# Two-layer streaming encoder: the slots of the weights' high and low parts at eight different residues of 128 bytes

## Chip, cores, metric

The kernel runs on one core of a Trainium2 chip. The metric is the device time of one execution in microseconds; lower is better.

## What is computed

The reference runs 1024 frames of width 1024, in float32, through two layers. The parts that take nearly all the time are products of activations with weights:

```python
h = h + mixer_ab(rmsnorm(h, g1), w_in, rel_a, sinks, w_out, t5_bias)   # layer 0: two kinds of chunked attention
h = h + dense_swiglu(rmsnorm(h, g2), wg, wu, wd)                       # 1024 -> 2816 -> 1024
h = h + mixer_c(rmsnorm(h, g1), w_in, vg, ws, bs, w_out)               # layer 1: gated unit with spatial mixing
h = h + moe_swiglu(rmsnorm(h, g2), wr, weg, weu, wed)                  # top 2 of 8 experts, 1024 -> 3584 -> 1024
return rmsnorm(h, final_norm)

def dense_swiglu(h, w_gate, w_up, w_down):
    return (jax.nn.silu(h @ w_gate) * (h @ w_up)) @ w_down
```

## The kernel before

**Split products.** Every float32 factor of a large product is split into a high part, rounded to `float32r`, and a low part, what the rounding left. A product is then three matmuls: high by high, high by low, low by high. `product` (line 306) writes them; all its matmuls carry line 314. Where its output is 512 columns wide and `wide` is not set, it does 256 columns at a time, and every matmul loads its stationary operand anew.

**Weights in units.** All weights come as units of 128 x 1024 floats. Four slots hold them: `wraw[:, j]` (as loaded), `wh[:, j]` (high part) and `wl[:, j]` (low part), j = 0 to 3. Unit u goes to slot u % 4. SyncE loads two slots at a time into `wraw` (`load_units`, line 286) once their low parts are made. ScalarE copies `wraw` to `wh` with rounding (`hi_part`, line 293, record at line 297), after the DMA and after TensorE is done with the unit that was in the slot (`unit_used`). VectorE subtracts (`lo_part`, line 299, record at line 301) and raises `lo_done`, for which TensorE waits before it uses the unit. There are 884 units in this run: 208 of the main weights and 676 of the experts.

**Who uses a unit, and how.**
- Projections (`half_pe` line 480, `out_unit_pe` line 855, `gate_up_pe` line 1120, `down_pe` line 1171): a tile of 128 x 128 of `wh` or `wl` is the stationary operand, and 240 to 512 columns of activations stream. These activations are `xs` (normalised input), `ah`/`al` (dense hidden), `exh`/`exl` (an expert's input) and `mah`/`mal` (an expert's hidden).
- The values of attention (`values_pe`, line 461) and of the gated unit (`mix_pe`, line 1290): 512 columns of `wh` or `wl` stream, and a tile of `xs` is stationary.
- The spatial mixing (in `mix_pe`) multiplies `wsh`/`wsl` with `vgh`/`vgl` by the same `product`, with 128 columns, and uses no unit.

**The stages in time.** Attention and its projections; output projection; dense layer in two halves of 512 frames (66 units each, 48 matmuls for each unit); gated unit; routing; then the items of the experts. An item is the frames of one expert, here eight of them, in rising order of size, each padded to a width out of `WIDTHS` (here three of 240, two of 256, two of 288, one of 304). An item takes 84 units: 56 for gate and up, 14 and 14 for the two halves of down, with 24 matmuls each.

**The allocation.** The tensors lie one behind the other in each partition. `wraw` begins at byte 16512, `wh` at 32896 and `wl` at 49280, all multiples of 128, and a slot has 4096 bytes. Then follow `ident`, `ones`, `gains` and other small ones, and from byte 67392 (64 past a multiple of 128) the large activations. `xs`, `ah`, `al`, `exh`, `exl`, `mah`, `mal`, `vgh`, `vgl`, `wsh` and `wsl` all begin 64 past a multiple of 128, and every slice that a matmul of line 314 takes keeps that. `eA` begins 64 past such a multiple too; `eB` begins 96 past one, and its second head 1028 bytes behind the first. Both are transposed with `ident` (lines 588 and 611).

Of the kernel before, what the change touches and what calls it, by code (L numbers as in the profile page):

```python
# [7 lines left out]
F32 = mybir.dt.float32  # L8
F32R = mybir.dt.float32r
U32 = mybir.dt.uint32  # L10
I32 = mybir.dt.int32
ALU = mybir.AluOpType
ACT = mybir.ActivationFunctionType
AX = mybir.AxisListType

P = 128
# [19 lines left out]
WIDTHS = (240, 256, 272, 288, 304, 336, CAP)  # L36
PIECES = -(-T // CAP)
NCAND = PIECES * NE
ROWS = 8
SLOTS = 2 * T + CAP  # L40


def t5_onehot():
# [15 lines left out]
def build(nc, io):  # L59
    ctx = ExitStack()  # L60
    with ctx:
        def sem(name):
            return ctx.enter_context(nc.semaphore(name))

        def sb(name, shape, dt=F32, scope=ctx):
            return scope.enter_context(nc.sbuf_tensor(name, shape, dt))


        wraw = sb("wraw", [P, 4, 1024])
        wh = sb("wh", [P, 4, 1024], F32R)  # L70
        wl = sb("wl", [P, 4, 1024], F32R)
        ident = sb("ident", [P, P])
        ones = sb("ones", [P, P])
        gains = sb("gains", [P, 4, KD])
# [4 lines left out]
        gate = sb("gate", [P, 2, NT])  # L79
        slot = sb("slot", [P, 2, NT], U32)  # L80
        tokl = sb("tokl", [P, CAP // P], U32)
        itab = sb("itab", [1, 3, NCAND + 1], I32)
        nitem = sb("nitem", [1, 1], I32)
        upto = sb("upto", [1, len(WIDTHS) + 1], I32)
        ps = ctx.enter_context(nc.psum_tensor("ps", [P, 8 * 512], F32))

        def bank(b, n=512, off=0):
# [80 lines left out]
        s4 = ExitStack()  # L168
# [25 lines left out]
        gt = sb("gt", [P, 3, NT], F32, s4)  # L194
        zlist = sb("zlist", [P, SLOTS // P], U32, s4)
        cand = sb("cand", [1, 6, NCAND], F32, s4)
        icnt = sb("icnt", [1, NCAND + 1], F32, s4)
        itf = sb("itf", [1, 3, NCAND + 1], F32, s4)
        s4.close()

        s4 = ExitStack()
# [5 lines left out]
        s4 = ExitStack()  # L207
# [5 lines left out]
        s4 = ExitStack()  # L213
# [5 lines left out]
        s4 = ExitStack()  # L219
# [17 lines left out]
        hrow_d = nc.dram_tensor("hrow_d", [T, D], F32)  # L237
        yrow_d = nc.dram_tensor("yrow_d", [SLOTS, D], F32)
        tok_d = nc.dram_tensor("tok_d", [SLOTS, 1], U32)
        extA_d = nc.dram_tensor("extA_d", [8, EXT_A], F32)  # L240
# [7 lines left out]
        hi_done, lo_done = sem("hi_done"), sem("lo_done")  # L248
# [44 lines left out]
        def hi_part(act, q, j):  # L293
            act.wait_ge(raw[j], 16 * q + 16)
            if not (isinstance(q, int) and q == 0):
                act.wait_ge(unit_used, 4 * q + j - 3)
            act.activation(wh[:, j], wraw[:, j], ACT.Copy).then_inc(hi_done, 1)  # L297

        def lo_part(dve, q, j):
            dve.wait_ge(hi_done, 4 * q + j + 1)  # L300
            dve.tensor_tensor(wl[:, j], wraw[:, j], wh[:, j].bitcast(F32),  # L301
                              ALU.subtract).then_inc(lo_done, 1)

        COLS = 256
# [367 lines left out]
        def first_act(act):  # L672
            act.wait_ge(tab_st, 80)
            for t in (0, 2):
                act.wait_ge(v_mm, t + 1)
                act.activation(vA[:, t], bank(t), ACT.Copy).then_inc(v_even, 1)
            for j in range(3):
                hi_part(act, 1, j)
            for t in (4, 6):
                act.wait_ge(v_mm, t + 1)  # L680
                act.activation(vA[:, t], bank(t), ACT.Copy).then_inc(v_even, 1)
            hi_part(act, 1, 3)
            half_act(act, U_KB, 0, 0)
            half_act(act, U_KB, 1, 1)
            hi_part(act, 2, 0)
            act.wait_ge(first_half, 2)
            act.activation(vbT[:, 0:HALF], bank(2), ACT.Copy).then_inc(pj_hi, 1)
            hi_part(act, 2, 1)
            half_act(act, unit_of(0, QA), 0, 4)
            act.wait_ge(vb_tr, 1)  # L690
            act.activation(vB[:, 0:4], bank(0).rearrange("p (t d) -> p t d", d=P), ACT.Copy).then_inc(vb_cp, 1)
            half_act(act, unit_of(0, KA), 0, 5)
            act.wait_ge(sink_in, 16)
            sink_act(act, 0)
            exps_a_act(act, 0)
            half_act(act, unit_of(0, QB), 0, 6)
            exps_b_act(act, 0)

        def first_dve(dve):
            dve.wait_ge(tab_st, 80)  # L700
            for t in (1, 3):
                dve.wait_ge(v_mm, t + 1)
                dve.tensor_copy(vA[:, t], bank(t)).then_inc(v_odd, 1)
            for j in range(3):
                lo_part(dve, 1, j)
            for t in (5, 7):
                if t == 5:
                    dve.wait_ge(v_mm, t + 1)
                else:
                    dve.wait_ge(unit_used, 4)  # L710
                dve.tensor_copy(vA[:, t], bank(t)).then_inc(v_odd, 1)
            lo_part(dve, 1, 3)
            half_dve(dve, U_KB, 0, 0, 0)
            half_dve(dve, U_KB, 1, 1, 1)
            lo_part(dve, 2, 0)
            dve.wait_ge(unit_used, U_VB + 1)
            dve.tensor_copy(vbT[:, HALF:T], bank(3)).then_inc(pj_lo, 1)
            lo_part(dve, 2, 1)
            half_dve(dve, unit_of(0, QA), 0, 4, 3)
            dve.wait_ge(vb_tr, 1)  # L720
            dve.tensor_copy(vB[:, 4:8], bank(1).rearrange("p (t d) -> p t d", d=P)).then_inc(vb_cp, 1)
            half_dve(dve, unit_of(0, KA), 0, 5, 4)
            least_a_dve(dve, 0)
            share_a_dve(dve, 0)
            half_dve(dve, unit_of(0, QB), 0, 6, 5)
            least_b_dve(dve, 0)
            share_b_dve(dve, 0)
# [991 lines left out]
        def item_act(act, it, n, base):  # L1719
            q = it * TURNS_E + Q_MOE  # L1720
            f0 = it * NF_E + F0
            gate_up_act(act, q, 0, NF_E, n, mah, f0, mst)
            d0, d1 = down_e(0), down_e(1)
            feed_act(act, q + d0[0], d0[1], NF_E // 2 - 1)
            copy_y_act(act, it, 0, n)
            turn_x_act(act, it + 1)
            feed_last_act(act, q + d0[0], d0[1], NF_E // 2)
            rows_y_act(act, it, 0, n, base)
            feed_act(act, q + d1[0], d1[1], NF_E // 2 - 1)
            copy_y_act(act, it, 1, n)  # L1730
            feed_last_act(act, q + d1[0], d1[1], NF_E // 2)
            rows_y_act(act, it, 1, n, base)
# [132 lines left out]
        def _(pool):  # L1865
# [75 lines left out]
            with pool.Fori(0, n_items) as it:  # L1941
                base = pool.value_load(itab[0:1, 1, bass.ds(it + 1, 1)], min_val=0, max_val=SLOTS - CAP)
                pool.wait_ge(xt_mm, 8 * it + 8)
# [26 lines left out]
        def _(act):  # L1970
# [24 lines left out]
            def item(it, n):  # L1995
                base = act.value_load(itab[0:1, 1, bass.ds(it, 1)], min_val=0, max_val=SLOTS - CAP)
                item_act(act, it, n, base)
# [112 lines left out]
```

## Time and profile before

| | before |
|---|---|
| time, median of 3 runs | 3727.32 us (3726.42 to 3730.49) |
| span of the profiled execution | 3722.7 us |
| PE busy | 3575.3 us, 96% |
| weight loads (PEld) busy | 3469.0 us, 93% |
| VectorE busy | 1769.7 us, 48% |
| ScalarE busy | 1672.4 us, 45% |
| GpSimd busy | 106.4 us, 3% |
| matmuls, weight loads | 29176 each |

The span runs from the first to the last instruction of one profiled execution; the median of the timed runs is 4.6 us longer. A busy share is not a rate: matmuls are pipelined, so several are shown as running at once, and how fast TensorE goes is seen from how many matmuls a stretch holds.

### The profile page before, as it was taken

The numbers are of one execution on the slowest core, as the hardware profiler recorded it, in microseconds if no ns is written. First come the engines' busy times: TensorE is split into PE (matmuls) and PEld (weight loads), VectorE is DVE, ScalarE is ACT, GpSimd is POOL, SyncE is SP. The second block draws the span as 40 slices with busy tenths as digits, with TensorE's granted clock in tenths as the row PEclk, the third lists the DMA queues.
The fourth block names the chain that finished last, engine by engine and source line by source line (L and its number), as shares of the span: only waits on it lengthen the run. The fifth ranks groups of instructions, "written<-read, shape, count | busy, mean of one in ns | idle before, by whom it ended". The sixth has DMA issues, their size and how long they took to land.

```text
span 3722.7 us, 76289 instructions
## 1 busy us (share of the span) xinstructions
PE 3575.3 (96%) x29176; PEld 3469.0 (93%) x29176; DVE 1769.7 (48%) x2532; ACT 1672.4 (45%) x2324; POOL 106.4 (3%) x137
## 2 busy tenths in 40 slices
PE   7999899999999999979999999999999999999993
PEld 5888799999999989879999999999999999999993
DVE  4455543333333455355555555555554444444444
ACT  3355533332333333346465564655644544544542
POOL 1000000000000000020000000000000000000001
PEclk9999999999999999979999999999999999999997
DMA  5111333333333322275666666566664555554446
GB/s 179 35 49 38 132 94 92 96 91 113 96 92 95 119 91 91 85 204 191 207 195 197 202 198 205 188 195 200 195 203 154 166 178 164 163 176 158 157 156 237
DMA packets 155604, 546.82 MB, mean 147 GB/s; under 512 B 18408, under 2 KB 18448, under 8 KB 155488
## 3 DMA queue, kind: packets, MB, share of 16 engines
q1 hardware_dynamic: 129744, 472.44, 40.0%
q0 software_dynamic: 16464, 55.52, 4.3%
q10 hardware_dynamic: 9280, 17.24, 1.2%
q8 instruction: 82, 1.34, 0.2%
q14 instruction: 34, 0.28, 0.0%
HBM read 515.51 MB, written 33.28 MB: 147 GB/s over the span
## 4 chain that ended last, share of the span: by engine, by line
PE 93%; DVE 3%; issue 1%; ACT 1%; DMA 1%; POOL 0%; ACTq 0%; DVEq 0%; POOLq 0%
PE ps L314 89%; DVE exl L1661 1%; PE ps L603 1%; PE ps L588 1%; PE ps L542 1%; PE ps L363 0%; DMA y<-yrow_d,slot 0%; PE ps L611 0%; PE ps L623 0%; PE ps L982 0%; PE ps L566 0%; DVE wl L301 0%; PE ps L1003 0%; ACT eA L662 0%; DMA yT<-in_xT 0%
## 5 line engine op out<-in xcount | busy, mean ns | idle before, releaser
L301 DVE TENSOR_TENSOR wl<-wraw,wh 128x1024 fp32r<-128x1024 f32 x884 | 1081.9, 1225 | 1442.6 <-ACT wh L297 1439.6
L297 ACT ACTIVATE wh<-wraw 128x1024 fp32r<-128x1024 f32 x884 | 929.4, 1057 | 1045.3 <-PE ps L314 1031.0
L314 PE MATMUL ps<-exh,wh 128*128 128x240 f32 (+3 forms) x3584 | 1020.6, 285 | 12.0 <-issue 9.8
L314 PE MATMUL ps<-exl,wh 128*128 128x240 f32 (+3 forms) x3584 | 1021.0, 285 | 0.0
L314 PE MATMUL ps<-exh,wl 128*128 128x240 f32 (+3 forms) x3584 | 1017.4, 284 | 0.0
L314 PE MATMUL ps<-xs,wh 128*128 128x256 f32 x5248 | 835.4, 282 | 2.4 <-DVE qAl L649 2.0
L314 PEld LDWEIGHTS ps<-xs,wh 128*128 128x128 f32 x5248 | 710.4, 190 | 12.5 <-issue 8.5
L314 PEld LDWEIGHTS ps<-exh,wh 128*128 128x128 f32 x3584 | 676.8, 189 | 13.1 <-issue 13.1
L314 PEld LDWEIGHTS ps<-exh,wl 128*128 128x128 f32 x3584 | 678.1, 189 | 0.0
L314 PEld LDWEIGHTS ps<-exl,wh 128*128 128x128 f32 x3584 | 677.7, 189 | 0.0
L314 PE MATMUL ps<-xs,wl 128*128 128x256 f32 x2624 | 521.6, 281 | 0.0
L314 PE MATMUL ps<-mah,wh 128*128 (+4 forms) x1792 | 510.4, 285 | 2.5 <-DVE exl L1661 2.5
L314 PE MATMUL ps<-mal,wh 128*128 (+4 forms) x1792 | 509.9, 285 | 0.0
L314 PE MATMUL ps<-mah,wl 128*128 (+4 forms) x1792 | 509.1, 284 | 0.0
L314 PEld LDWEIGHTS ps<-xs,wl 128*128 128x128 f32 x2624 | 402.5, 189 | 0.0
L314 PEld LDWEIGHTS ps<-mah,wh 128*128 128x128 f32 x1792 | 337.8, 189 | 4.4 <-issue 4.4
L314 PEld LDWEIGHTS ps<-mah,wl 128*128 128x128 f32 x1792 | 338.2, 189 | 0.0
L314 PEld LDWEIGHTS ps<-mal,wh 128*128 128x128 f32 x1792 | 337.5, 188 | 0.0
L1148 ACT ACT_TABLE_LOAD x134 | 171.9, 1283 | 303.5 <-PE ps L314 284.6
L314 PE MATMUL ps<-ah,wh 128*128 (+1 forms) x704 | 141.2, 282 | 0.0
L314 PE MATMUL ps<-al,wh 128*128 (+1 forms) x704 | 140.5, 281 | 0.0
L314 PE MATMUL ps<-ah,wl 128*128 (+1 forms) x704 | 140.5, 281 | 0.0
(293 smaller groups left out, 2805.8 us busy)
## 6 DMA issues: line engine op xcount, KB each, us to landing
wraw<-in_w_expert SPq DMA_DIRECT2D x676, 512.0 KB
wraw<-in_w_main SPq DMA_DIRECT2D x208, 512.0 KB
yrow_d<-yst ACTq DMA_DIRECT2D x16, 512.0 KB
yT<-in_xT POOLq DMA_DIRECT2D x4, 1024.0 KB, 11.3
hT<-in_xT POOLq DMA_DIRECT2D x2, 2048.0 KB, 9.8
h_d<-hT POOLq DMA_DIRECT2D x2, 2048.0 KB, 9.9
hT<-h_d POOLq DMA_DIRECT2D x2, 2048.0 KB, 13.6
xrow_d<-rows ACTq DMA_DIRECT2D x16, 256.0 KB, 2.2
```

Source lines behind the costliest of these rows:

```text
L297: act.activation(wh[:, j], wraw[:, j], ACT.Copy).then_inc(hi_done, 1)
L301: dve.tensor_tensor(wl[:, j], wraw[:, j], wh[:, j].bitcast(F32), ALU.subtract).then_inc(lo_done, 1)
L314: mm = pe.matmul(out[:, s], a, b[:, s], start=first and part == 0 and c == 0, stop=last and part == 2 and c + w == n)
L542: mm = pe.matmul(ps[:, starts[h] + a * P:starts[h] + b * P], (qAh, qAh, qAl)[part][hp, tc], key, start=part == 0, stop=part == 2)
L588: mm = pe.transpose(ps[:, o:o + P], eA[:, h, kk * P:kk * P + P], ident[:])
L603: mm = pe.matmul(Y_OUT[h * HD:h * HD + HD], v, ptA[:, kk, h], start=kk == 0, stop=kk == na - 1)
L1148: act.activation(buf[:, par, 0:n], bank(b + par, n), ACT.Silu).then_inc(silu_done, 1)
L1661: dve.scalar_tensor_tensor(exl[:, k], bank(k % 4, CAP), gains[:, 3, k:k + 1], exh[:, k].bitcast(F32), ALU.mult, ALU.subtract).then_inc(x_l ...
```

## The change

The slots of `wh` and `wl` get a pitch of 1032 columns in place of 1024, that is 4128 bytes, and `wl` begins 4 columns (16 bytes) later than the allocation would put it. So the slots of `wh` begin at 0, 32, 64 and 96 bytes past a multiple of 128, and those of `wl` at 16, 48, 80 and 112. `wraw` stays at 4096 bytes per slot. The added bytes are made up for: the three tables of items (`itab`, `nitem`, `upto`) move into a region that is free at that time, and a filler `fill` brings the activations to the same addresses as before. `ident`, `ones`, `gains`, `epsc`, `gate`, `slot` and `tokl` begin 288 bytes higher, `vstat` too. The instructions, their order on every engine, their waits and their sizes are the same.

```diff
+SKEW = 8
...
         wraw = sb("wraw", [P, 4, 1024])
-        wh = sb("wh", [P, 4, 1024], F32R)
-        wl = sb("wl", [P, 4, 1024], F32R)
+        wh = sb("wh", [P, 4, 1024 + SKEW], F32R)
+        wl_all = sb("wl", [P, SKEW // 2 + 4 * (1024 + SKEW)], F32R)
+        wl = wl_all[:, SKEW // 2:].rearrange("p (j c) -> p j c", j=4)
...
-        itab = sb("itab", [1, 3, NCAND + 1], I32)
-        nitem = sb("nitem", [1, 1], I32)
-        upto = sb("upto", [1, len(WIDTHS) + 1], I32)
+        sb("fill", [P, 24])
...
         itf = sb("itf", [1, 3, NCAND + 1], F32, s4)
+        itab = sb("itab", [1, 3, NCAND + 1], I32, s4)
+        nitem = sb("nitem", [1, 1], I32, s4)
+        upto = sb("upto", [1, len(WIDTHS) + 1], I32, s4)
...
-            act.activation(wh[:, j], wraw[:, j], ACT.Copy).then_inc(hi_done, 1)
+            act.activation(wh[:, j, 0:1024], wraw[:, j], ACT.Copy).then_inc(hi_done, 1)
...
-            dve.tensor_tensor(wl[:, j], wraw[:, j], wh[:, j].bitcast(F32),
+            dve.tensor_tensor(wl[:, j, 0:1024], wraw[:, j], wh[:, j, 0:1024].bitcast(F32),
                               ALU.subtract).then_inc(lo_done, 1)
```

## Rows read from the trace of the kernel before

**Rows 1.** The page: span, and busy time of each engine.
```profile
span 3722.7 us, 76289 instructions
PE 3575.3 (96%) x29176; PEld 3469.0 (93%) x29176; DVE 1769.7 (48%) x2532; ACT 1672.4 (45%) x2324; POOL 106.4 (3%) x137
```

**Rows 2.** The page: the chain that ended last, by engine and by line.
```profile
PE 93%; DVE 3%; issue 1%; ACT 1%; DMA 1%; POOL 0%; ACTq 0%; DVEq 0%; POOLq 0%
PE ps L314 89%; DVE exl L1661 1%; PE ps L603 1%; PE ps L588 1%; PE ps L542 1%; PE ps L363 0%; DMA y<-yrow_d,slot 0%; PE ps L611 0%; PE ps L623 0%; PE ps L982 0%; PE ps L566 0%; DVE wl L301 0%; PE ps L1003 0%; ACT eA L662 0%; DMA yT<-in_xT 0%
```

**Rows 3.** PE's waits (total us, times, longest); line 314's idle time for `wl`.
```profile
PE ps L1650 <- DMA xg<-xrow_d,tokl: 11.9, 1, 11.9
PE ps L314 <- issue: 9.8, 2, 6.3
...
  DVE wl L301: 2.2, 2
```

**Rows 4.** The page's groups: busy us, mean ns | idle before, and its releaser.
```profile
L301 DVE TENSOR_TENSOR wl<-wraw,wh 128x1024 fp32r<-128x1024 f32 x884 | 1081.9, 1225 | 1442.6 <-ACT wh L297 1439.6
L297 ACT ACTIVATE wh<-wraw 128x1024 fp32r<-128x1024 f32 x884 | 929.4, 1057 | 1045.3 <-PE ps L314 1031.0
```

**Rows 5.** Windows, line 314 alone: us, busy with counts, granted clock, DMA share, GB/s.
```profile
440.00:470.00 30.00, 30.00 (x267) 30.00 (x267) 1.00 0.57 205
600.00:700.00 100.00, 100.00 (x852) 100.00 (x850) 1.00 0.31 94
1000.00:1100.00 100.00, 100.00 (x851) 100.00 (x850) 1.00 0.32 93
1300.00:1340.00 40.00, 40.00 (x176) 32.83 (x175) 1.00 0.39 119
1480.00:1500.00 20.00, 20.00 (x179) 20.00 (x178) 1.00 0.38 111
1700.00:1750.00 50.00, 50.00 (x444) 50.00 (x443) 1.00 0.61 193
1900.00:2000.00 100.00, 100.00 (x896) 100.00 (x895) 1.00 0.62 194
2400.00:2450.00 50.00, 50.00 (x444) 50.00 (x443) 1.00 0.62 196
2778.00:2798.00 20.00, 20.00 (x172) 20.00 (x172) 1.00 0.70 241
2900.00:2950.00 50.00, 50.00 (x377) 50.00 (x376) 1.00 0.50 165
3450.00:3500.00 50.00, 50.00 (x363) 50.00 (x362) 1.00 0.49 159
```

**Rows 6.** Lines 297 and 301 by themselves: shortest, median and longest ns.
```profile
L297 ACT ACTIVATE wh<-wraw x884: 1039/1060/1082, 4.7 to 3662.4; 128x1024 fp32r<-128x1024 f32 x177
L301 DVE TENSOR_TENSOR wl<-wraw,wh x884: 1203/1226/1248, 13.5 to 3663.5; 128x1024 fp32r<-128x1024 f32 x177
```

**Rows 7.** Timeline, PE in the attention: start us, us, four transposes each.
```profile
140.75 0.66 PE L588 MATMUL ps<-ident,eA 128*128 128x128 f32 x4
146.13 0.66 PE L611 MATMUL ps<-ident,eB 128*128 128x128 f32 x4
```

**Rows 8.** Groups with shapes kept apart and the page's groups: how many of which.
```profile
L314 PE MATMUL ps<-xs,wh 128*128 128x256 f32 x5248 | 835.4, 282 | 2.4 <-DVE qAl L649 2.0
L314 PE MATMUL ps<-xs,wl 128*128 128x256 f32 x2624 | 521.6, 281 | 0.0
L314 PE MATMUL ps<-ah,wh 128*128 (+1 forms) x704 | 141.2, 282 | 0.0
L314 PE MATMUL ps<-exh,wh 128*128 128x240 f32 x1344 | 371.9, 277 | 3.5 <-issue 3.5
L314 PE MATMUL ps<-exh,wh 128*128 128x256 f32 x896 | 247.7, 276 | 1.1 <-DVE wl L301 1.1
```

**Rows 9.** Groups of weight loads in windows 600 to 700 and 2900 to 2950.
```profile
L314 PEld LDWEIGHTS ps<-xs,wh 128*128 128x128 f32 x566 | 77.2, 190 | 0.0
L314 PEld LDWEIGHTS ps<-xs,wl 128*128 128x128 f32 x284 | 43.3, 188 | 0.0
...
L314 PEld LDWEIGHTS ps<-exh,wh 128*128 128x128 f32 x125 | 23.5, 188 | 0.0
```

**Rows 10.** Groups of weight loads in window 1411 to 1420, beside the spatial products.
```profile
L314 PEld LDWEIGHTS ps<-xs,wh 128*128 128x128 f32 x40 | 5.3, 188 | 0.0
L314 PEld LDWEIGHTS ps<-wsh,vgl 128*128 128x128 f32 x7 | 1.3, 192 | 0.0
```

## Prediction

> **What bounds the kernel now.** I read the page first, then the chain of waits, then the windows over single stages, then the groups by shape. The reader is to see one thing: TensorE sets the time, and it sets it by the spacing of its matmuls, not by waiting. PE is busy for 3575.3 us of the 3722.7 us span [rows 1]; the chain that ended last is PE for 93%, and line 314, the products with `wh` and `wl`, alone is 89% [rows 2]. PE's waits are small: the largest is 11.9 us, and for `wl` it waits only 2.2 us in all of line 314 [rows 3]. VectorE spends 1442.6 us idle before the low parts and ScalarE 1045.3 us before the high parts [rows 4], so both are fed late because TensorE frees slots late, and neither limits it.
>
> Now the spacing. A window over a stretch that is full of one shape gives it: length divided by the count (a matmul is shown for about 0.28 us, so about two of each count began before the window; I take them off). All windows used stand at a granted clock of 1.00, that is 2.4 GHz [rows 5]:
> - 256 columns: 100 us / 850 = 117.7 ns in the dense layer (windows 600 and 1000), 117.6 ns at 2778, but 113.0 to 113.2 ns at 440, 1480 and 2400;
> - 240 columns: 113.1 ns in the first such item (1700), 111.9 ns in the next (1900);
> - 288 columns 133.3 ns, 304 columns 138.5 ns, 512 columns 229.9 ns.
>
> So **the same shape has two speeds, 4.5 ns apart**, in stages with the same kind of operands at the same addresses modulo 128. Something small in how a weight load and a running matmul meet costs a few ns each time, on some 27,000 matmuls. That is all this change can touch, and 1 ns on each of them would be 27 us, 0.7%.
>
> **The change part by part.** The profiled execution has a span of 3722.7 us; the median of the runs is 3727.32 us, 4.6 us above it. I make the sum against the span and add those 4.6 us.
>
> *Order and work.* No instruction is added, removed or moved on any engine, and each keeps its shape, its waits and its number of elements. DMA into `wraw` is untouched. Cost: 0.
>
> *High and low parts on ScalarE and VectorE.* The 884 copies into `wh` (1057 ns each) and 884 subtractions into `wl` (1225 ns each) [rows 4] write, and the second also reads, at other addresses. The spread over the whole kernel is 1039 to 1082 ns and 1203 to 1248 ns [rows 6], with every slot in it, so position among the slots gives at most some 45 ns. If every subtraction took even 5% more (61 ns), 884 of them are 54 us, and they lie inside the 1442.6 us of idle time; PE would see it only where it waits for `wl` today, 2.2 us [rows 3]. I take 0, between 0 and 1 us. If that cover went, the low part would be late for PE, unit by unit.
>
> *The small constants.* `ident`, `ones`, `gains` and the router's tables move up by 288 bytes and the tables of items to a far place. They are used by few, short instructions. `ident` is the moving operand of the transposes. I take 0 for all of them.
>
> *The matmuls.* Here is the only real term. By the allocation, `wraw`, `wh` and `wl` now all begin at a multiple of 128 bytes, and all other operands of line 314 (`xs`, `ah`, `exh`, `mah`, their low halves, and all their slices) at 64 bytes past one. So today every weight load of this line stands 64 bytes (mod 128) from the operand that streams meanwhile, except in the spatial products. With the change the high slots stand at 0, 32, 64, 96 and the low ones at 16, 48, 80, 112: in seven of eight cases the relation is another. The trace holds no row with any of those relations at 256 columns, so I bound the cost. The nearest row for a weight load that begins on no round address is the transposes of `eB`: its second half begins 1028 bytes in, 4 bytes past a multiple of 16. Four of them take 0.66 us, exactly as long as four transposes of `eA`, which begin at 64 past a multiple of 128 [rows 7]. So an odd start alone costs nothing visible there (those have 128 columns, and both streams run at one rate). The nearest rows for what the meeting can cost are the two speeds of 256 columns: 4.5 ns to either side. From the counts [rows 8], 256 columns occur 6336 times in the dense layer (4224 of the 7872 with `xs`, and 3 x 704 with `ah`, `al`) and 672 times in the late half of the down products of two items: about 7010 at the slow speed. The rest, 3648 with `xs` and 3360 in the items, is about 7010 at the fast one (a part of the attention's is slow too). Then there are 6048 of 240 columns, and 4032 + 2016 of 288 and 304. Lower end: the 7010 of the dense layer's pace take the quicker one, -7010 x 4.5 = -31.5 us, and the 6048 wide ones gain 4.5 ns too, -27 us: -58 us. Upper end: the other 7010 take the dense layer's pace, +31.5 us, the wide ones lose as much, +27 us: +58 us. I take 0, as in the transposes, since that is the only row where just the start differs; both ends stay for the range.
>
> The 4.5 ns step shows also in the weight loads: 190 ns on average for `wh` in the slow window (two lengths), 188 ns for the others and at 288 columns [rows 9]. That two streams with unchanged relation fall into either speed speaks for timing inside TensorE rather than for addresses.
>
> The page of the Trainium skill "TensorE: Matmul & The Clock Gate" (section "Wait — 56ns, not 53.3ns?") gives N/2.4 + 2.5 ns, 109.2 ns for 256 columns; the windows show 113 to 118 ns, so the measurement decides and something beyond the page's rule is paid here. By the page, were the excess a clash that the change removes, the sum would be some 140 us lower, about 3590 us.
>
> Sum: 3722.7 + 0 + 0 + 0 + 4.6 = **3727 us**.
>
> **The rivals.**
> *A. Addresses do matter, and the mix is kinder (faster).* The dense layer leaves its slow speed when the relation changes with each unit of weights. For: 7010 matmuls sit 4.5 ns above what the same shape does elsewhere [rows 5], so there is room. Against: the dense layer kept 117.7 ns through 132 units and all waits, so units do not reset it. Time: 3727 - 31.5 = 3696 us; down to 3669 us if the wide ones gain too.
> *B. Addresses do matter, and 64 was a good relation (slower).* Each unit of 24 or 48 matmuls now has its own relation; the place is the 7010 fast 256-column products in the output projections, the gated unit and the items, and the price 4.5 ns each: 3727 + 31.5 = 3759 us, up to 3786 us with the wide ones. It decides as soon as more matmuls lose their 113 ns than the dense layer wins it. For: the spatial products, the only ones of line 314 whose two operands both stand at 64, show weight loads of 192 ns where the others mostly show 188 [rows 10]. Against: they have 128 columns, so their meeting is another.
> *C. The matmuls' reads do not clash at all.* This is my forecast's mechanism. The Trainium skill, "SBUF — State Buffer", section "Who interferes with whom", gives TensorE two independent read ports and says PE never waits on anyone; by that rule the change does nothing, and the excess in rows 5 stays. No run here shows the ports.
> *D. The change does not do what it says.* The skew could be lost if slots were padded; but 1032 columns of 4 bytes are 4128 bytes, 32 past a multiple of 128, so it is there.
>
> **How the numbers follow.** A measurement of this kernel can tell about 0.2%, 7.5 us, from no change. Forecast (no change, the excess is timing within TensorE) 0.40; A 0.34, of which 0.06 goes below 3670 us; B 0.26, of which 0.06 goes above 3780 us. A stands above B because the slow speed is the one the longest stage is in. A mixture that cancels to within 7.5 us is counted with the forecast. The range takes both bounds of the matmul term, 3670 to 3780 us, and leaves out a little over 1 in 10; the forecast's own range is 3720 to 3735 us. Chances: faster 0.34, the same 0.40, slower 0.26.
>
> **What would show it.** Right: the same counts in the same windows, 850 per 100 us in the dense layer, 442 per 50 us at 2400, 375 at 2900; weight loads of 188 and 192 ns in the same stages; copies and subtractions within 1% of 1057 and 1225 ns. Rival A: over 870 matmuls in 100 us of the dense layer. Rival B: under 435 in 50 us of the 256-column items. If addresses matter, the spacing should change from one slot to the next within a stage, in steps of 24 or 48 matmuls; that pattern, or a busy DVE that PE waits for, would prove me wrong.

## The result, and the profile after

The changed kernel takes 3741.22 us (median of 4 runs, 3739.99 to 3743.82), the kernel before, run beside it, 3726.87 us (4 runs, 3720.55 to 3730.49). The ratio is 1.0043, with a 95% interval of 1.003 to 1.0057. The change costs 14 us here. (Beside the later experiments the kernel before had medians of 3719.16 to 3721.21 us, with single runs from 3702.62 to 3733.02; experiment 11, which runs as the change does, came out 21 us above it, at 1.0054.) That is inside the range, but it is not "no change": the forecast was wrong, and what came true is the mechanism of rival B, at half its price.

The page of the kernel after: span, busy times, the chain by engine, and the two groups that write the slots. Every line number of the products is three higher now, 317 in place of 314.

```profile
span 3739.2 us, 76289 instructions
...
PE 3593.6 (96%) x29176; PEld 3485.7 (93%) x29176; DVE 1769.9 (47%) x2532; ACT 1675.0 (45%) x2324; POOL 106.0 (3%) x137
...
PE 93%; DVE 3%; issue 1%; ACT 1%; DMA 1%; ACTq 0%; POOL 0%; SPq 0%; DVEq 0%; POOLq 0%
...
L304 DVE TENSOR_TENSOR wl<-wraw,wh 128x1024 fp32r<-128x1024 f32 x884 | 1081.8, 1224 | 1453.2 <-ACT wh L300 1451.6
L300 ACT ACTIVATE wh<-wraw 128x1024 fp32r<-128x1024 f32 x884 | 931.1, 1058 | 1058.0 <-PE ps L317 1047.1
```

The span grew by 16.5 us, PE's busy time by 18.3 us [rows 1], with the same instructions. The parts on ScalarE and VectorE take what they took, 1058 and 1224 ns against 1057 and 1225 [rows 4]; they only wait longer, by 11 us (VectorE) and 13 us (ScalarE). So the time is in TensorE's spacing. Windows over line 317 alone, with the same columns as in [rows 5]:

```profile
440.00:470.00 30.00, 30.00 (x257) 30.00 (x256) 1.00 0.52 180
600.00:700.00 100.00, 100.00 (x854) 100.00 (x853) 1.00 0.30 94
...
1480.00:1500.00 20.00, 20.00 (x173) 20.00 (x172) 1.00 0.37 108
1700.00:1750.00 50.00, 50.00 (x448) 50.00 (x447) 1.00 0.64 196
1900.00:2000.00 100.00, 100.00 (x894) 100.00 (x893) 1.00 0.62 193
2400.00:2450.00 50.00, 50.00 (x427) 50.00 (x426) 1.00 0.60 192
2900.00:2950.00 50.00, 50.00 (x379) 50.00 (x379) 1.00 0.50 167
3450.00:3500.00 50.00, 50.00 (x359) 50.00 (x358) 1.00 0.47 157
```

Against [rows 5], the 256-column products at 440, 1480 and 2400 have lost: 267 became 257, 179 became 173, 444 became 427. The dense layer has won two matmuls in 100 us (852 to 854). 288 columns (377 to 379) have won a little, 304 columns (363 to 359) have lost. 240 columns have more at 1700 (444 to 448) and fewer at 1900 (896 to 894): the first item of the kernel before ran at 113.5 ns, its two others at 112.0, and the change has 111.9 to 112.3 ns in all three. So no position has won there, the kernel before only had one item at a slower pace. The granted clock is 1.00 in every one of these rows, before and after, so it is not the clock.

What that is worth by stage can be read off the chain of waits, since PE's long pieces begin most stages (start us, length us, what; 2880 matmuls are the last 7 units of the output projection, behind the sum of squares of its norm, and the first 53 of the dense layer, 1680 an item's first 70 units). The kernel after:

```profile
482.10 338.18 PE ps L317 x2880
...
1626.94 190.31 PE ps L317 x1680
...
2333.80 198.18 PE ps L317 x1680
...
2833.22 225.75 PE ps L317 x1680
...
3389.50 235.74 PE ps L317 x1680
```

The same view of the kernel before:

```profile
483.81 339.20 PE ps L314 x2880
...
1625.71 192.97 PE ps L314 x1680
...
2334.33 190.72 PE ps L314 x1680
...
2817.90 226.03 PE ps L314 x1680
...
3375.89 233.24 PE ps L314 x1680
```

| stretch, between the starts above | before us | after us | difference |
|---|---|---|---|
| start to that sum | 483.8 | 482.1 | -1.7 |
| 7 units of the output projection, dense layer, gated unit, routing | 1141.9 | 1144.8 | +2.9 |
| three items of 240 | 708.6 | 706.9 | -1.8 |
| two items of 256 | 483.6 | 499.4 | +15.9 |
| two items of 288 | 558.0 | 556.3 | -1.7 |
| item of 304 and the end | 346.8 | 349.7 | +2.9 |

The two items of 256 columns carry the loss. How much of such a table is chance shows in a second profile of the kernel before (experiment 8): its first stretch is 5.8 us shorter than here, its items of 256 take 5.1 us longer (488.6 us), and the other stretches agree within 0.5 us. So the -1.7 us of the first stretch means nothing, and against that profile the items of 256 would have lost 10.8 us. One piece of 1680 matmuls there took 190.72 us, 113.5 ns each, and now takes 198.18 us, 118.0 ns each: the step of 4.5 ns between the two paces that the prediction had seen.

The sign that the prediction named for "addresses matter" is there too. These are the records of PE on line 317 in four windows of 5.0 us, inside four consecutive units of the dense layer, in slots 0, 1, 2, 3 of the kernel after (count: shortest/median/longest ns, first and last start):

```profile
L317 PE MATMUL ps<-xs,wh x32: 276/276/279, 634.2 to 639.4; 128*128 128x256 f32 x32
...
L317 PE MATMUL ps<-xs,wh x31: 279/281/283, 639.7 to 644.9; 128*128 128x256 f32 x31
...
L317 PE MATMUL ps<-xs,wh x30: 274/281/287, 645.4 to 650.5; 128*128 128x256 f32 x30
...
L317 PE MATMUL ps<-xs,wh x30: 278/281/297, 651.1 to 656.2; 128*128 128x256 f32 x30
```

Slot 0 alone shows 276 ns, the others 281 ns, and this repeats every four units. As the mean distance from one matmul's start to the next within a unit, and of that the median over the 132 units of the layer, slots 0 to 3 have 114.6, 118.5, 118.0 and 118.5 ns; before, all four had 117.8 ns. Other traffic doesn't explain it: windows of 5.2 us in the same four units hold 47, 46, 46, 46 matmuls, here the first three, with the DMA share in the last column but one:

```profile
634.30:639.50 5.20, 5.20 (x47) 5.20 (x47) 1.00 0.35 100
639.90:645.10 5.20, 5.20 (x46) 5.20 (x46) 1.00 0.03 12
645.60:650.80 5.20, 5.20 (x46) 5.20 (x46) 1.00 0.58 176
```

so an almost silent and a busy DMA (0.03 and 0.58) give the same count.

### The profile page after: what moved, and what is told of

Same layout as the page of the kernel before. It is cut to its first block, busy times and chain, and to the rows that moved or that the text cites. A ratio compares the mean times of both kernels' runs of the same rounds, so it can differ in the third digit from the quotient of the medians.

```text
span 3739.2 us, 76289 instructions
## 1 busy us (share of the span) xinstructions
PE 3593.6 (96%) x29176; PEld 3485.7 (93%) x29176; DVE 1769.9 (47%) x2532; ACT 1675.0 (45%) x2324; POOL 106.0 (3%) x137
## 4 chain that ended last, share of the span: by engine, by line
PE 93%; DVE 3%; issue 1%; ACT 1%; DMA 1%; ACTq 0%; POOL 0%; SPq 0%; DVEq 0%; POOLq 0%
PE ps L317 89%; DVE exl L1664 1%; PE ps L606 1%; PE ps L591 1%; PE ps L545 1%; PE ps L626 0%; PE ps L366 0%; PE ps L985 0%; PE ps L614 0%; DMA hr<-hrow_d 0%; DVE wl L304 0%; PE ps L569 0%; ACT eA L665 0%; PE ps L1006 0%; DVE y L1781 0%
## 5 line engine op out<-in xcount | busy, mean ns | idle before, releaser
L304 DVE TENSOR_TENSOR wl<-wraw,wh 128x1024 fp32r<-128x1024 f32 x884 | 1081.8, 1224 | 1453.2 <-ACT wh L300 1451.6
L300 ACT ACTIVATE wh<-wraw 128x1024 fp32r<-128x1024 f32 x884 | 931.1, 1058 | 1058.0 <-PE ps L317 1047.1
```

Of the source, the lines that this page charges most:

```text
L300: act.activation(wh[:, j, 0:1024], wraw[:, j], ACT.Copy).then_inc(hi_done, 1)
L304: dve.tensor_tensor(wl[:, j, 0:1024], wraw[:, j], wh[:, j, 0:1024].bitcast(F32), ALU.subtract).then_inc(lo_done, 1)
```

## Experiments

**Theories at the start.** The first: the pace depends on where the weights begin relative to the streamed operand, and the change is slower because its places are worse. Its rival: the matmuls don't care, and something else that moved (the 288 bytes under `ones` and `ident`, the tables) or chance in how TensorE falls into one of two paces makes the 14 us.

What each version does to the allocation, in bytes past a multiple of 256 (the activations that stream begin at 64 in every version):

| | high slots | low slots | `ones`, past 128 |
|---|---|---|---|
| before | 128 | 128 | 0 |
| the change | 128, 160, 192, 224 | 16, 48, 80, 112 | 32 |

Between the two, the low slots also moved by 128 bytes, because the longer `wh` pushes them on. The diff doesn't show it at a glance, and it turned out to count.

Most experiments are made from the change by one edit, which keeps the room of both tensors and everything behind them in its place:

```diff
-        wh = sb("wh", [P, 4, 1024 + SKEW], F32R)
+        wh_all = sb("wh", [P, 4 * (1024 + SKEW)], F32R)
+        wh = wh_all[:, 0:4096].rearrange("p (j c) -> p j c", j=4)
         wl_all = sb("wl", [P, SKEW // 2 + 4 * (1024 + SKEW)], F32R)
-        wl = wl_all[:, SKEW // 2:].rearrange("p (j c) -> p j c", j=4)
+        wl = wl_all[:, 0:4096].rearrange("p (j c) -> p j c", j=4)
```

This is the first of them, `e1_slots_back`: every slot is 4096 bytes again, the high ones at 128 and the low ones at 0 past a multiple of 256. For the others only the two slices are shown, as a difference to it.

**1. No skew at all.** 

> The slots of the high and low weights are back at multiples of 128 bytes; the small constants stay 288 bytes higher and the tables of items stay moved (the low slots begin 128 bytes later than before). Theory R (the spacing of TensorE's matmuls depends on how the weight tile and the streaming operand stand to each other modulo 128 bytes): the time of the kernel before, 3727 us within 4 us, 113.3 ns for 256 columns in the items, 117.8 ns in the dense layer. Theory S (the side moves of ident, ones, gains and tables cost the 14 us): about 3741 us, and 117.8 ns in the 256-column items.

Measured: 3678.49 us (6 runs, 3675.59 to 3679.22), ratio to the kernel before 0.9889 (0.9871 to 0.9907). It is 41 us quicker than the kernel before (3719.67 us beside it), and its span is 62 us shorter than that of the change; both theories had missed it. Windows over its products (line 318), then its chain of waits:

```profile
600.00:700.00 100.00, 100.00 (x885) 100.00 (x884) 1.00 0.30 94
2400.00:2450.00 50.00, 50.00 (x443) 50.00 (x443) 1.00 0.59 190
2900.00:2950.00 50.00, 50.00 (x383) 50.00 (x383) 1.00 0.52 168
3450.00:3500.00 50.00, 50.00 (x359) 50.00 (x358) 1.00 0.46 154
```

```profile
479.50 326.44 PE ps L318 x2880
...
1591.81 189.81 PE ps L318 x1680
...
2296.69 190.70 PE ps L318 x1680
...
2777.50 223.07 PE ps L318 x1680
...
3327.34 235.48 PE ps L318 x1680
```

The dense layer runs at 885 per 100 us, 113.3 ns, where before and change both have some 852. Against the kernel before, by the same stretches as in the table: start -4.3, from the sum to routing -29.6, items of 240 -3.7, of 256 -2.8, of 288 -8.2, of 304 with the end +2.8, together -45.8 us, which is the difference of the spans (3676.9 and 3722.7). So the skew itself costs 62 us, and the kernel before had a loss of its own, which had to be found.

**2. Only the low slots, 16 bytes on.**

```diff
-        wl = wl_all[:, 0:4096].rearrange("p (j c) -> p j c", j=4)
+        wl = wl_all[:, 4:4100].rearrange("p (j c) -> p j c", j=4)
```

> All four high slots at 0, all four low slots at 16 bytes past a multiple of 128: slot 0 of the change, for every slot. Theory R: every slot shows what slot 0 of the change shows: about 114.6 ns in the dense layer (117.8 before), 112.2 ns at 240 columns, 117.8 ns in the 256-column items, 133.6 at 288, 139.3 at 304; in total 6336 x 3.2 = 20 us won in the dense layer and about 15 us lost in the items of 256 columns, so about 3720 us. Theory H (a stage falls into one of two paces by how it was entered, and addresses only push it): no prediction by slot; the dense layer may stand at either 113 or 118 ns, and the change's slot 0 need not be found again.

Measured: 3733.53 us (10 runs, 3726.67 to 3737.3), ratio 1.0036 (1.0023 to 1.0048). Sixteen bytes on one tensor cost 55 us against experiment 1. 852 matmuls in 100 us of the dense layer, 423 in 50 us at 2400. Slot 0 of the change stands at the very same bytes and has 114.6 ns in the dense layer, where this version has 117.8: the position doesn't fix the pace alone, as the text behind the table of positions shows.

**3. Both skewed, without the 16 bytes.**

```diff
+        wh = wh_all[:, 0:4128].rearrange("p (j c) -> p j c", j=4)
+        wl = wl_all[:, 0:4128].rearrange("p (j c) -> p j c", j=4)
```

> High and low slots both at 0, 32, 64, 96, without the extra 16 bytes of the low ones. Theory R: slot 0 is then as before (both at 0) and shows 117.8 ns in the dense layer in place of the 114.6 of the change, slots 1 to 3 near the change's 118.5, 118.0, 118.5; about 3745 us. If the 16 bytes between high and low are what costs (theory L): the 256-column items go back to 113.3 ns and the time to 3727 us or below.

Measured: 3737.24 us (6 runs, 3734.34 to 3739.94), ratio 1.0046 (1.003 to 1.0063). Dense spacing by slot: 113.3, 117.8, 120.0, 119.4 ns. Slot 0, which stands exactly as in experiment 1, has its pace; the three that are moved lose it. The spacing follows the unit's own address, four units at a time, within one stage of one execution: that rules out the constants and the tables as the cause of the difference between slots.

**4. Both 64 bytes on.**

```diff
+        wh = wh_all[:, 16:4112].rearrange("p (j c) -> p j c", j=4)
+        wl = wl_all[:, 16:4112].rearrange("p (j c) -> p j c", j=4)
```

> All slots, high and low, at 64 bytes past a multiple of 128, where the streaming activations stand too (relation 0, as in the spatial products). Theory R with 64 apart as a good relation: slower than before in every stage, 256 columns at 118 ns and up throughout, 3755 to 3790 us. Theory H: every slot alike in each stage, some stages at 113 and some at 118 ns, 3700 to 3760 us.

Measured: 3742.65 us (4 runs, 3740.64 to 3745.11), ratio 1.0064 (1.0041 to 1.0088). High and low keep their distance to each other as in experiment 1, and only their place, and with it the distance to the streamed operand, changes; 64 us are lost. All slots begin at the same residue of 128 bytes as the activations, which does not help. So it is no matter of high against low alone.

**5 to 7. Which 128 bytes.** Experiment 1 and the kernel before have the same residues of 128 for all slots, yet differ by 41 us. Three versions ask what is left: the low slots exactly where they were before (made from the change, `wh` and the start of `wl` as before, the constants and tables as in the change), the low slots 256 bytes further than that, and both tensors at a multiple of 256.

```diff
-        wh = sb("wh", [P, 4, 1024 + SKEW], F32R)
-        wl_all = sb("wl", [P, SKEW // 2 + 4 * (1024 + SKEW)], F32R)
-        wl = wl_all[:, SKEW // 2:].rearrange("p (j c) -> p j c", j=4)
+        wh = sb("wh", [P, 4, 1024], F32R)
+        wl_all = sb("wl", [P, 4164], F32R)
+        wl = wl_all[:, 0:4096].rearrange("p (j c) -> p j c", j=4)
```

> As e1_slots_back, but the low slots also back at byte 49280, where they were before; only the small constants (288 bytes up) and the tables of items differ from the kernel before. Theory C (the constants won the 41 us of e1_slots_back): about 3680 us and 113.3 ns in the dense layer. Theory P (the place of the low slots 128 bytes on won them): the kernel before again, about 3720 us, 117.8 ns in the dense layer, 133.2 ns at 288 columns. Theory H (a stage falls into either of two paces by accident of timing, at the same addresses): neither by rule.

Measured: 3690.76 us (10 runs; eight between 3683.11 and 3697.16, two at 3714.91 and 3716.48), ratio 0.9929 (0.9906 to 0.9952).

```diff
+        wl = wl_all[:, 32:4128].rearrange("p (j c) -> p j c", j=4)
```

> High slots at byte 32896, low slots at 49536, 256 bytes past their place before and 128 past that of e1_slots_back; constants as there. Theory P with a period of 256 bytes: as the kernel before, 117.8 ns in the dense layer, about 3720 us. If it is period 512 or more, or only the distance of 16384 bytes between high and low that hurts: as e1_slots_back, 113.3 ns and about 3680 us, or a pace of its own. Theory C: 3680 us.

Measured: 3686.12 us (4 runs, 3684.81 to 3695.6), ratio 0.991 (0.9882 to 0.9938).

```diff
+        wh = wh_all[:, 32:4128].rearrange("p (j c) -> p j c", j=4)
```

> High slots at byte 33024 and low ones at 49408: both 128 bytes on, again 16384 bytes apart as before. If the distance of 16384 between high and low sets the slower pace: about 3720 us and 117.8 ns in the dense layer. If it is the relation of the low slots to the streaming operand at a period above 128 (theory P): as e1_slots_back or with a pace of its own, since the high ones moved too. Theory C: 3680 us.

Measured: 3730.34 us (10 runs, 3725.31 to 3734.35), ratio 1.0022 (1.0009 to 1.0035). High and low are as far apart as in the kernel before and in experiment 5, and the time is 40 us above experiment 5: the distance between the two doesn't set it.

Windows over the products at 600, 2900 and 3450 us, of the version with the low slots at their old place:

```profile
600.00:700.00 100.00, 100.00 (x885) 100.00 (x884) 1.00 0.33 95
2900.00:2950.00 50.00, 50.00 (x378) 50.00 (x377) 1.00 0.51 167
3450.00:3500.00 50.00, 50.00 (x363) 50.00 (x362) 1.00 0.48 157
```

and of the one 256 bytes further:

```profile
600.00:700.00 100.00, 100.00 (x885) 100.00 (x884) 1.00 0.32 94
2900.00:2950.00 50.00, 50.00 (x377) 50.00 (x376) 1.00 0.52 167
3450.00:3500.00 50.00, 50.00 (x363) 50.00 (x362) 1.00 0.48 157
```

The counts are the same within one. Experiment 1, which differs from the latter by 128 bytes in the low slots only, has 383 at 2900 and 359 at 3450. So shifting the low slots by 256 bytes changes nothing in these windows and by 128 bytes it does: **what counts is the address modulo 256**, not 128. (The two profiles do differ in the first projections of the attention, 113.3 and 117.8 ns, and in the second item of 240, 112.0 and 113.3 ns. The next experiment shows such differences between two profiles of one kernel.) And a riddle appeared: the low slots at their old place have 885 per 100 us in the dense layer, where the kernel before has 852 [rows 5] with `wh`, `wl` and all activations at the same bytes.

**8. The kernel before, unchanged, with a new profile.** 

> The kernel before, unchanged, with a profile of its own. If addresses alone set the pace: the same pace in every stage as in the first profile, 117.8 ns in the dense layer, 133.3 at 288 columns, 113.3 in the 256-column items. Theory H: at least one stage at the other pace, and a time that differs from 3722.7 us by some 5 to 30 us.

Measured: 3724.56 us, one run. Its windows over line 314:

```profile
600.00:700.00 100.00, 100.00 (x851) 100.00 (x851) 1.00 0.31 94
2400.00:2450.00 50.00, 50.00 (x426) 50.00 (x426) 1.00 0.55 178
```

The dense layer is at 851 again, so that is a trait of this kernel. But at 2400 there are 426 where the first profile had 444 [rows 5]: the same program, the same addresses, the same item, and the other pace. In this execution the second half of that item's down products then ran at 113.3 ns, in the first it ran at 117.8. So at this position 256 columns have two paces, and which is taken isn't fixed by the addresses of the two operands.

**9. `ones` back at a multiple of 128.** Of what still differed between the kernel before and the version with the low slots at their old place, the place of the small constants is the candidate. Where does the kernel before change its pace? Windows over line 314 right before and after the sum of squares of the output projection's norm, and the timeline between them:

```profile
460.00:470.00 10.00, 10.00 (x91) 10.00 (x90) 1.00 0.28 91
490.00:500.00 10.00, 10.00 (x87) 10.00 (x86) 1.00 0.32 79
```

```profile
482.79 1.02 PE L398 MATMUL ps<-acc,ones 128*128 128x512 f32 x2
```

91 in 10 us up to the two matmuls with `ones`, 87 after them. From start to start the last products before them stand 112 to 114 ns apart, and from the first behind them on 116 to 119 ns. The edit moves `ones`, and with it the small tensors behind it, up by 96 bytes, made from the version with the low slots at their old place:

```diff
+        sb("fill", [P, 24])
         ones = sb("ones", [P, P])
...
-        sb("fill", [P, 24])
```

> As e7_low_at_old_place, with ones and the small tensors behind it 96 bytes further, so that ones begins at a multiple of 128 again, as in the kernel before; ident stays 288 bytes up. In the kernel before TensorE goes from 113.3 to 117.8 ns at the sum with ones in the output projection, and stays so through the dense layer. Theory O (where ones stands decides at which pace the stream goes on after that sum): 117.8 ns in the dense layer, about 3720 us. Theory C (ident or the others): 113.3 ns and about 3690 us as in e7. If the pace is only a draw: times of both kinds in about equal numbers.

Measured: 3718.56 us (12 runs, 3713.19 to 3728.06), ratio 0.9997 (0.9987 to 1.0008): the time of the kernel before, 28 us above the same kernel with `ones` 96 bytes lower. Its products (line 317) behind the sum:

```profile
490.00:500.00 10.00, 10.00 (x87) 10.00 (x86) 1.00 0.33 107
600.00:700.00 100.00, 100.00 (x851) 100.00 (x850) 1.00 0.31 94
```

**10. The other way round: the kernel before, with `ones` 32 bytes on.** The small tensors behind `ones` move with it; no slot and no activation moves, nor does `ident`.

```diff
         ident = sb("ident", [P, P])
+        sb("skip", [P, 8])
         ones = sb("ones", [P, P])
...
-        itab = sb("itab", [1, 3, NCAND + 1], I32)
-        nitem = sb("nitem", [1, 1], I32)
-        upto = sb("upto", [1, len(WIDTHS) + 1], I32)
+        sb("fill", [P, 88])
```

> The kernel before with ones and the small tensors behind it 32 bytes on (tables of items moved as in the change to make room); slots, ident and activations stay. Theory O (the sum with ones sets the pace at which the output projection's second half and the dense layer go on): 113.3 ns in the dense layer, about 3690 us, 0.8% below the kernel before. If ident has a part in it: 117.8 ns and about 3720 us.

Measured: 3689.39 us (6 runs, 3686.11 to 3698.14), ratio 0.9922 (0.9902 to 0.9942), 30 us under the kernel before. Its windows over line 316, and the timeline:

```profile
460.00:470.00 10.00, 10.00 (x91) 10.00 (x90) 1.00 0.37 105
490.00:500.00 10.00, 10.00 (x91) 10.00 (x90) 1.00 0.28 86
600.00:700.00 100.00, 100.00 (x885) 100.00 (x884) 1.00 0.31 94
```

```profile
478.91 1.02 PE L400 MATMUL ps<-acc,ones 128*128 128x512 f32 x2
```

The two matmuls with `ones` take 1.02 us in both kernels. They cost the same by themselves; behind them the products keep the pace of 91 in 10 us instead of falling to 87, through the last 336 of the output projection and the 6336 of the dense layer: 6672 x 4.5 ns = 30.0 us. Experiments 9 and 10 show cause and place from both directions. Of what moved with `ones`, `epsc` and `gains` are read in this norm only behind the sum, when the pace of the products has already changed, and the others belong to later stages; so `ones` is left. (In this version the three tables of items lie in the free region, as in the change; experiment 9 has them there too and has the time of the kernel before, so they are not it.)

**11. The same on the change.** The edit of experiment 9, on the changed kernel.

> The change, with ones (and the small tensors behind it) 96 bytes further, at a multiple of 128 as in the kernel before. If the place of ones only chooses between two paces that a stage has, and the skewed slots leave the dense layer no such choice (each slot has its own pace, 114.6, 118.5, 118.0, 118.5 ns): the change's time, 3735 to 3745 us, and the same four paces. If it acts as in e7 against e11: 20 to 30 us slower than the change, about 3765 us.

Measured: 3740.55 us (5 runs, 3739.13 to 3742.77), ratio 1.0054 (1.0034 to 1.0074); the change has 3741.22. 853 per 100 us in the dense layer, 427 per 50 us at 2400. With skewed slots the place of `ones` is worth nothing.

**12, 13. One tensor skewed, the other not.** For the high slots alone, then for the low slots alone:

```diff
+        wh = wh_all[:, 0:4128].rearrange("p (j c) -> p j c", j=4)
```

> e1_slots_back with the four high slots at 0, 32, 64, 96, the low ones all at a multiple of 256. Theory R (each position of weights against the streaming operand modulo 256 has its own set of paces, and most positions lack the 113.3 ns of 256 columns): slot 0 stays at 113.3 ns in the dense layer or the items, slots 1 to 3 at 117 to 121 ns; about 3725 us. If only the low slots matter (one load in three): 3680 us.

```diff
+        wl = wl_all[:, 0:4128].rearrange("p (j c) -> p j c", j=4)
```

> e1_slots_back with the four low slots at 0, 32, 64, 96 past a multiple of 256, the high ones all where they were before. Theory R: slots 1 to 3 lose the 113.3 ns too, since 16 bytes on the low slots alone cost 55 us against e1 (e2_low_at_16): 3710 to 3735 us. If only the high slots matter (two loads in three): 3680 us.

Measured: 3726.01 us (10 runs, 3724.18 to 3730.87), ratio 1.0015 (1.0005 to 1.0025), and 3727.61 us (10 runs, 3723.0 to 3731.73), ratio 1.0021 (1.0008 to 1.0035). Both have 857 in 100 us of the dense layer and 431 in 50 us at 2400. Against experiment 1 each costs 47 to 49 us, the two together (experiment 3) 59 us: they don't add up. One of the two tensors out of place is nearly enough to spoil a slot.

**14. The low slots 64 bytes on, the high ones where they were.**

```diff
+        wl = wl_all[:, 16:4112].rearrange("p (j c) -> p j c", j=4)
```

> High slots as before, all low slots at 64 past a multiple of 256, the same residue as the streaming activations. Theory R: a uniform pace in every slot of a stage; 256 columns at 117 to 119 ns like the case with all slots at 64, since low loads then meet their operand at relation 0: 3710 to 3740 us. If it keeps the 113.3 ns and has the 131 ns of e1 at 288 columns, it is as good as e1, 3680 us or below.

Measured: 3745.55 us (4 runs, 3744.78 to 3750.92), ratio 1.0069 (1.0049 to 1.0089), the longest of all.

```profile
600.00:700.00 100.00, 100.00 (x851) 100.00 (x851) 1.00 0.30 94
...
2900.00:2950.00 50.00, 50.00 (x377) 50.00 (x376) 1.00 0.51 164
3450.00:3500.00 50.00, 50.00 (x365) 50.00 (x364) 1.00 0.47 154
```

It has neither the quicker pace at 256 columns nor experiment 1's at 288, but the best of all at 304: 365 in 50 us.

**All uniform positions and the change side by side**, as the mean distance in ns between the starts of two matmuls within a unit, of that the median over a stage's units (streamed operand at 64 in each):

| high, low (past a multiple of 256) | kernels | dense, 256 columns | items of 256 | of 288 | of 304 |
|---|---|---|---|---|---|
| 128, 128 | before, 5, 6, 8, 9, 10 | 113.3 or 117.8 | 113.3 or 117.8 | 133.2 to 133.5 | 138.7 |
| 128, 0 | 1 | 113.3 | 113.3 | 131.1 | 140.0 |
| 128, 16 | 2 | 117.8 | 119.0 and 117.8 | 131.2 to 133.2 | 139.5 |
| 128, 64 | 14 | 117.8 | 117.8 | 133.4 | 137.7 |
| 0, 0 | 7 | 117.8 | 117.8 | 131.6 to 132.2 | 137.9 |
| 192, 64 | 4 | 117.7 | 118.3 | 132.2 | 138.9 |
| the change, slots 0 to 3 | change, 11 | 114.6, 118.5, 118.0, 118.5 | 117.7, 117.9, 117.9, 117.5 | 133.6, 131.1, 133.3, 133.0 | 139.2, 141.4, 138.7, 141.2 |

A row isn't a law of its position. At (128, 16) the output projection up to the sum with `ones`, and the gated unit, run at 114.5 ns, as slot 0 of the change does; with the first product behind the sum the pace is 117.8, although `ones` stands 32 bytes on as in experiment 1, where it stays at 113.3. So 256 columns have at least three paces there (114.5, 117.8, 119.0), and of the 55 us of experiment 2 some 21 us (6336 x 3.3 ns) are the dense layer's choice among them. At (128, 64) the last 13 units of one item run at 122.4 ns. Of the uniform positions all but (128, 128) have one profile only, so a cell with one number may hide a second pace.

## Why the prediction was wrong

*Order and work, 0.* Right: the same 76289 instructions, and every stage difference is one of spacing.

*High and low parts, 0.* Right: 1058 and 1224 ns against 1057 and 1225 [rows 4], and PE waits for a low part as little as before [rows 3]:

```profile
  DVE wl L304: 2.2, 2
```

*The small constants, 0.* This step failed in the kernel before, though not in the change. "They are used by few, short instructions" is true, and the conclusion isn't: the place of `ones` under two matmuls of 1.02 us decides the pace of the 6672 that follow, 30 us (experiments 9 and 10). In the changed kernel it decides nothing (experiment 11), so this step isn't what the sum missed. But the 32 bytes by which the change moved `ones` would have brought 30 us had the slots stayed.

*The matmuls, 0 between -58 and +58.* This is **the step of the sum that failed**. It measured +16.5 us. "I take 0, as in the transposes, since that is the only row where just the start differs": the row was too far away. The transposes of [rows 7] have 128 columns and come four at a time; nothing in them shows what a sustained train of loads and matmuls does. The bounds, made from the step of 4.5 ns and the counts of [rows 8], held.

*"That two streams with unchanged relation fall into either speed speaks for timing inside TensorE rather than for addresses."* The observation was right, and the new profile of the same kernel shows it even for the same item (experiment 8). The "rather than" was wrong. Both hold: the position of the weights modulo 256, with the activations at 64, sets which paces exist (experiments 1 to 7, 14), and at (128, 128) what ran just before chooses between two of them in the dense layer (9, 10). Two speeds at one address are no evidence that addresses don't matter. A row hinted at it, though weakly, since its width differs too: the spatial products, with both operands at 64, whose weight loads took 4 ns more than the rest [rows 10]. The length of the weight loads was no sign of the pace: in the change's dense layer, at about 118 ns, their mean is 188 ns, as at 113.3 ns.

*Rival A (3696 us, the dense layer leaves its pace).* Its reserve is real: experiment 1 and experiment 10 have the dense layer at 113.3 ns, and 30 us less. But the skew doesn't fetch it; it gives slot 0 most of it (114.6 ns) and makes the three others slightly worse, which leaves 2.3 us (6336 x 0.36 ns).

*Rival B (3759 us, the quicker 256-column products lose their pace).* This happened, in the items of 256 and at 440 and 1480 us, at just the 4.5 ns. The price was halved because B counted 7010 matmuls and not all of them lost. The items' 3360 lose in full (3360 x 4.5 = 15.1 us, measured 15.9). The gated unit and its projections lose in part, since slot 0 keeps 114.6 ns there: the stretch up to routing grows by 2.9 us although the dense layer in it wins 2.3. Most of the 2112 of the attention and the output projection had no such pace to lose: from unit 7 to 29 of these the mean distance is 148 to 182 ns before, because waits and other matmuls of the attention stand between, and 12 more units ran at 117.8 already, 5 at the start and the 7 behind the sum with `ones`. The 304 columns lose 2.9 us; the 288 columns, which B's longer time of 3786 us had losing, win 1.7.

*Rival C, the forecast's mechanism.* The Trainium skill, "SBUF — State Buffer", section "Who interferes with whom", has TensorE reading through two independent ports and never waiting on anyone. Sixteen bytes in one operand's start that cost 55 us (experiment 2) don't fit a reading of it by which the place of the two operands is free, as the forecast took it. Here the measurement decides; no run shows the ports themselves. The Trainium skill, "TensorE: Matmul & The Clock Gate", section "Wait — 56ns, not 53.3ns?", gives N/2.4 + 2.5 ns, by an estimate from it 109.2 ns for 256 columns; the best position found has 113.3 ns, so the measurement decides here too. Over the widths and counts of the prediction the excess above this rule is an estimated 210 us and not the 140 us that it names; the forecast doesn't use that number.

*Rival D.* The change does what it says; the pattern by slots proves it. What the text on the change left out is that the low slots also went 128 bytes on. It should have stood there, since 128 bytes count.

**What stays open.** Why a position has the paces it has: no rule was found that would give 131.1 ns for 288 columns at (128, 0) and 140.0 for 304. The activations began at 64 in every version, so nothing here tells whether the place of the weights counts by itself or against the streamed operand. How a matmul hands its pace on to the next is not shown, only that it does. Of the two runs at 3715 us of the version with the low slots at their old place no profile exists; a dense layer at 117.8 ns would give that time, but that is only argued.

The experiments did give a kernel that beats both: the one of experiment 1, 3678.49 us, 0.9889 (0.9871 to 0.9907) of the kernel before. It moves no slot against another and takes nothing away; its low slots stand 128 bytes on, and `ones` stands 32 bytes on.

## What to carry to other kernels

Where TensorE is bound by a train of weight loads and matmuls, count the matmuls of one shape in windows, stage by stage; where a shape has two paces, the start of the weights modulo 256 bytes is worth a sweep (that of the streamed operand may be, it wasn't tried), in whole steps for a whole tensor, because the skews tried here only mixed good places with bad ones. Take two profiles of one kernel before reading a stage's difference. When an edit to an allocation moves the time, list everything that it moved, the small constants too, and put each back by itself before naming a cause.

## What the runs showed of the hardware that was not expected

- The spacing of `float32r` products whose weights are loaded for each matmul depends on the weights' starts modulo 256 bytes, with the streamed operand at 64, all at a granted clock of 1.00: 113.3 to 122.4 ns at 256 columns, 131.1 to 133.6 at 288, 137.7 to 141.4 at 304. The three widths don't agree on the best position. Whole kernels differ by 67 us, from 3678.49 to 3745.55, by it and by the choice of pace.
- At one and the same position 256 columns have two stable paces, 113.3 and 117.8 ns at (128, 128); 240 columns have 112.0 and 113.5 there. TensorE kept one over the 6336 matmuls of the dense layer, across the bounds of units, and two matmuls with another operand switched it. At (128, 128) the place of that operand decided whether they did, and that was worth 30 us; at (128, 16) they did with `ones` 32 bytes on too.
